# A two-layer decoder trunk on one core: normalised tokens kept in the residual's column order, a shorter rank computation and finer filler units ahead of the expert stage

## The chip, the cores and the metric

The kernel runs on one core of one Trainium2 chip. The metric is the device time of the whole launch in microseconds (us), the median of several executions.

## What is computed

Two layers over 256 tokens of width 1024, batch 1. Each layer is a mixer (a gated short convolution beside block-sparse attention, which with 256 tokens is plain causal attention) and then a hierarchical mixture of experts. Only the second matters here. Cut to it:

```
h2 = rmsnorm(x, norm2_g[l]) * (1.0 + scale2) + shift2
g_logits = t @ w_rg + b_rg                      # 4 groups
g_sel    = argmax(g_logits)
e_logits = (t @ w_re + b_re).reshape(n, 4, 4)   # 4 experts in each group
top_v, top_i = top_k(e_logits[tok, g_sel], 2)
w_sel    = softmax(top_v) * g_prob[tok, g_sel]
hid = silu(t @ w_gate[e]) * (t @ w_up[e])       # D 1024 -> F 256, 16 experts
y   = sum over the chosen experts of combine * hid @ w_down[e]
x   = x + gate2 * y
```

All inputs and outputs are float32. Where two logits are equal, the lower index wins, in `argmax` and in `top_k`.

## The kernel before, in words

All weights are streamed once, in an order written out by hand (`stream`), through ten slots of 1 MB in SBUF (`raw`); SyncE issues the loads and waits before each for the slot's last reader (`wait_free`). Each layer runs: projections, attention, output projection, and then the router and the experts. Every engine has its own hand-written program, and semaphores tie them together.

**Router.** After the output projection, TensorE transposes the residual (`res_transposes`, line 1697; it takes every fourth column, stride 4, because the weight rows lie in SBUF as "partition p holds rows 4p to 4p+3 of a half"). It multiplies by the router weights (`router_rows`, line 1704) and adds four partial rows (line 1740). VectorE forms the logits `lg` (line 1228), compares all pairs in each set of four (lines 1234 to 1239), sums to ranks (line 1240) and gets the assignment `asg` (line 1245). TensorE turns `asg` into places (lines 1745, 1747, 1750) and VectorE builds the selection matrices `sel` (line 1256), 64 slots for each expert. Between these steps TensorE is given filler work, `late_units`: products of the modulation weights that must be done at some time anyway (line 1410 in layer 0, kind "A", eight units; line 1402 in layer 1, kind "G2", four units of twice the matmuls).

**Normalised tokens.** ScalarE writes the high part `xn_hi` (a rounded fp32r copy of the residual times its scale, line 717) and VectorE the low part `xn_lo` (what rounding left, line 1195). Both read the residual with a stride of 4 floats and write it permuted: the 128 columns of feature block k lie side by side. `xn_low(0, ...)` runs while row 1 of the residual is still being made; `xn_low(1, 0, 2)` stands behind the assignment, `xn_low(1, 1, 3)` behind the first quarter of `sel`.

**Experts.** Sixteen experts go in eight pairs. `gather(q, g)` (line 1766) multiplies the normalised tokens by `sel` to put the features of quarter q's tokens in columns. Its stationary operand is a 128x128 block of `xn_hi` or `xn_lo`, its moving operand 256 columns of `sel`:

```
ins = pe.matmul(ps[:, bank, j * S:(j + 1) * S], xn[part][:, t, k * P:(k + 1) * P],
                sel[:, t, 256 * q:256 * (q + 1)], ...)
```

One call is 8 matmuls; there are 16 calls in a layer, four in a row for quarter 0 and then one between the other steps of pairs 0 to 5. `gate_up` (line 1786), `hid_transpose` (line 1795), `down` (line 1812) and `scatter` (line 1828) make up the rest of a pair. ScalarE turns each gathered piece into `hg` (line 755). Before the first pair's second half come the transposes of `sel` (line 1854) and the combine weights (line 1863).

`ada_cols` (line 1445) is a small product whose stationary operand is a 128x128 float32 block of `mod_rows`: for kind "A" with columns side by side, for kind "M" with every fourth column (`mod_rows[:, j::4]`).

Of the kernel before, what the change touches and what calls it, by code (L numbers as in the profile page):

```python
# [13 lines left out]
P = 128  # L14
# [8 lines left out]
BIG = 4096.0  # L23
RING = 6
# [7 lines left out]
def trunk(nc, x, c, positions, norm1_g, norm2_g, w_ada, b_ada, w_in, conv_w, q_norm_g, k_norm_g,  # L32
# [31 lines left out]
    with ExitStack() as ctx:  # L64
# [371 lines left out]
        def _(pool):  # L436
# [15 lines left out]
            for i in range(1, EG):  # L452
                pool.memset(tri[:, i, 0:i], 1.0)
# [59 lines left out]
        def _(act):  # L513
# [103 lines left out]
            for l in range(L):  # L617
# [97 lines left out]
                def xn_high(t, h0, h1):  # L715
                    cols = slice(512 * h0, 512 * h1)
                    act.activation(xn_hi[:, t, cols].rearrange("p (h k q) -> p h k q", h=h1 - h0, k=4),
                                   res[:, t, cols].rearrange("p (h q k) -> p h k q", h=h1 - h0, k=4),
                                   ACT.Copy, scale=stat[:, t:t + 1]).then_inc(xhi_ready, 1)
# [112 lines left out]
        def _(dve):  # L832
# [165 lines left out]
            for l in range(L):  # L998
# [193 lines left out]
                def xn_low(t, h, n):  # L1192
                    cols = slice(512 * h, 512 * (h + 1))
                    dve.wait_ge(xhi_ready, 3 * l + n)
                    dve.scalar_tensor_tensor(out=xn_lo[:, t, cols].rearrange("p (k q) -> p k q", k=4),
                                             in0=res[:, t, cols].rearrange("p (q k) -> p k q", k=4),
                                             scalar=stat[:, t:t + 1],
                                             in1=xn_hi[:, t, cols].bitcast(F32).rearrange("p (k q) -> p k q", k=4),
                                             op0=ALU.mult, op1=ALU.subtract).then_inc(xlo_ready, 1)
# [25 lines left out]
                dve.tensor_copy(logit4[:, P:2 * P], ps[:, 0, 0:P]).then_inc(rows_dve, 1)  # L1225
                dve.wait_ge(logit_done, l + 1)
                for t in range(T):
# [6 lines left out]
                dve.tensor_tensor(beat, other, own, ALU.is_gt)  # L1234
                link(dve.tensor_tensor(tie, other, own, ALU.is_equal))
                link(dve.tensor_tensor(tie, tie,
                                       tri[:, :, :].unsqueeze(1).to_broadcast([P, T * (NG + 1), EG, EG]),
                                       ALU.mult))
                link(dve.tensor_tensor(beat, beat, tie, ALU.add))
# [10 lines left out]
                xn_low(1, 0, 2)  # L1250
# [3 lines left out]
                for q in range(NQ):  # L1254
                    es = slice(4 * q, 4 * q + 4)
                    dve.tensor_tensor(sel.rearrange("p t (e s) -> p t e s", s=SLOTS)[:, :, es, :],  # L1256
                                      slots[:, 0:SLOTS].unsqueeze(1).unsqueeze(1).to_broadcast([P, T, 4, SLOTS]),
                                      slot_of[:, :, es].unsqueeze(3).to_broadcast([P, T, 4, SLOTS]),
                                      ALU.is_equal).then_inc(sel_ready, 1)
                    if q == 0:  # L1260
                        xn_low(1, 1, 3)
# [125 lines left out]
        def _(pe):  # L1387
            def ada_acc(kind, l, ks):
# [6 lines left out]
                for k in ks:  # L1395
                    unit = ("a", q, k)
                    pe.wait_ge(raw_full[ring_slot[unit]], landed[unit])
                    if kind in ("G1", "G2"):
                        for j in range(2):
                            for i in range(4):  # L1400
                                c0 = j * D + 256 * i
                                ins = pe.matmul(ps[32 * i:32 * i + 32, 6, 0:256], c_rep[:, 2 * k + j, :],  # L1402
                                                raw[:, ring_slot[unit], c0:c0 + 256],
                                                start=(k == 0 and j == 0), stop=(k == 3 and j == 1),
                                                skip_group_check=True)
                        ins.then_inc(ada_used, 1)
                        continue
# [100 lines left out]
            def layer(l):  # L1508
# [199 lines left out]
                def late_units(first, last):  # L1708
                    if l + 1 < L:
                        ada_acc("A", l + 1, range(2 * first, 2 * last))  # L1710
                    else:
                        ada_acc("G2", l, range(first, last))
# [17 lines left out]
                res_transposes(1, 6, 8, 2)  # L1730
                pe.wait_ge(tokT_dve, l + 1)
# [3 lines left out]
                late_units(0, 1)  # L1735
# [7 lines left out]
                late_units(1, 3)  # L1743
# [9 lines left out]
                late_units(3, 4)  # L1753

                xn = (xn_hi, xn_lo)

                def gather(q, g):
# [4 lines left out]
                    for j in range(2):  # L1762
                        k = 2 * g + j
                        for t in range(T):
                            for part in range(2):
                                ins = pe.matmul(ps[:, bank, j * S:(j + 1) * S], xn[part][:, t, k * P:(k + 1) * P],  # L1766
                                                sel[:, t, 256 * q:256 * (q + 1)], start=(t == 0 and part == 0),
                                                stop=(t == T - 1 and part == 1))
# [124 lines left out]
                def every_expert():  # L1893
# [3 lines left out]
                    for k in range(KD):  # L1897
                        for t in range(T):
                            c0 = (k % 2) * S + t * P
                            ins = pe.transpose(ps[:, k // 2, c0:c0 + P], tokmaj[:, t, k * P:(k + 1) * P], ident[:, :])  # L1900
# [72 lines left out]
```

## Time and profile before

| | us |
|---|---|
| median of 3 runs | 551.92 (551.55 to 552.21) |
| the profiled execution's own time | 551.99 |
| its span, first to last instruction | 550.2 |
| TensorE matmul busy | 534.3 (97% of the span) |
| TensorE weight load busy | 346.6 (63%) |
| VectorE busy | 299.2 (54%) |
| ScalarE busy | 222.7 (40%) |
| moved from HBM | 188.12 MB, 344 GB/s over the span |
| mean granted TensorE clock | 0.994 |

Busy times of TensorE are modelled at their ends and overlap (a 256-column matmul is shown with 283 ns while the next starts 120 ns later). So the pace of TensorE is read here from start to start. The expert stages lie at about 161 to 285 us and 418 to 546 us.

### The profile page before, as it was taken

Reading aid. Unit: us, or ns where it says so; the run is one execution under the profiler, and the core shown is the slowest. Engines: PE = TensorE matmul, PEld = TensorE weight load, DVE = VectorE, ACT = ScalarE, POOL = GpSimd, SP = SyncE. Lnnn points to the kernel's source line nnn. Section 1 sums busy time; section 2 is a strip of 40 time slices with the busy share of each in tenths; the row PEclk is TensorE's granted clock in tenths of the full one; section 3 lists DMA queues with packets and bytes.
Section 4 is the critical chain, followed back from the end, with each engine's and each line's share of the span. In section 5 each row is a group of like instructions: output and inputs, shape, how many; then the busy total and the mean of one; then the engine's idle time right before and its main releaser. Section 6 shows DMA issues by size and latency. Waiting matters only on the chain.

```text
span 550.2 us, 8078 instructions
## 1 busy us (share of the span) xinstructions
PE 534.3 (97%) x3236; PEld 346.6 (63%) x3236; DVE 299.2 (54%) x502; ACT 222.7 (40%) x384; POOL 18.2 (3%) x76
## 2 busy tenths in 40 slices
PE   7799999999999999999999999999999999999996
PEld 6568969868755444444357898986875544444333
DVE  3628985899872012222369499499977121112243
ACT  2517555542445322222267365563255422222121
POOL 3104100000000000000000000000000000000000
PEclk9899999999999999999999999999999899999999
DMA  8999999979679999999999943956958799999962
GB/s 299 387 387 365 401 396 416 419 310 395 231 276 413 414 414 413 414 409 418 408 386 388 381 150 116 407 213 255 384 203 304 273 371 399 414 413 415 411 247 80
DMA packets 52222, 189.77 MB, mean 345 GB/s; under 512 B 4722, under 2 KB 4818, under 8 KB 44884
## 3 DMA queue, kind: packets, MB, share of 16 engines
q1 hardware_dynamic: 50784, 185.62, 86.6%
q0 software_dynamic: 1072, 2.45, 1.3%
q10 hardware_dynamic: 324, 1.13, 0.6%
q8 instruction: 28, 0.46, 0.3%
q14 instruction: 14, 0.11, 0.1%
HBM read 188.12 MB, written 1.06 MB: 344 GB/s over the span
## 4 chain that ended last, share of the span: by engine, by line
PE 82%; DVE 10%; ACT 3%; DMA 2%; issue 1%; SPq 1%; ACTq 0%; DVEq 0%
PE ps L1786 20%; PE ps L1543 13%; PE ps L1812 10%; PE ps L1664 8%; PE ps L1550 7%; PE ps L1766 5%; PE ps L1828 5%; PE ps L1410 4%; DMA raw<-in_w_ada_dram 2%; DVE wlo L852 2%; DVE cbc L1099 1%; PE ps L1795 1%; PE ps L1402 1%; SPq L352 1%; DVE work L1324 1%
## 5 line engine op out<-in xcount | busy, mean ns | idle before, releaser
L852 DVE TENSOR_TENSOR wlo<-raw,whi 128x1024 fp32r<-128x1024 f32 x64 | 75.6, 1219 | 15.8 <-ACT whi L547 15.5
L547 ACT ACTIVATE whi<-raw 128x1024 fp32r<-128x1024 f32 x64 | 65.3, 1058 | 24.4 <-PE ps L1543 14.3
L1324 DVE SCALAR_TENSOR_TENSOR work<-ps,cw,work 128x256 f32<-128x256 f32 x16 | 10.9, 682 | 97.5 <-ACT work L793 97.5
L1786 PE MATMUL ps<-raw,qkT 128*64 128x512 f32 x256 | 60.0, 612 | 0.0
L1310 DVE TENSOR_TENSOR v_sb<-ps,gates 128x512 f32<-128x512 f32 x32 | 22.1, 692 | 67.7 <-PE ps L1812 67.7
L1812 PE MATMUL ps<-raw,work 128*64 128x512 f32 x256 | 58.4, 598 | 0.0
L1786 PE MATMUL ps<-raw,cbc 128*64 128x512 f32 x256 | 57.5, 594 | 0.0
L1543 PE MATMUL ps<-act_hi,whi 128*128 128x256 f32 x192 | 55.0, 286 | 0.0
L1543 PE MATMUL ps<-act_hi,wlo 128*128 128x256 f32 x192 | 54.3, 283 | 0.0
L1543 PE MATMUL ps<-act_lo,whi 128*128 128x256 f32 x192 | 54.3, 283 | 0.0
L781 ACT ACTIVATE whi<-v_sb 128x512 fp32r<-128x512 f32 x32 | 20.2, 631 | 56.6 <-DVE v_sb L1310 56.6
L1786 PEld LDWEIGHTS ps<-raw,cbc 128*64 128x64 f32 x256 | 18.0, 137 | 34.8 <-issue 33.7
L1543 PEld LDWEIGHTS ps<-act_hi,whi 128*128 128x128 f32 x192 | 36.8, 192 | 2.5 <-issue 2.3
L1786 PEld LDWEIGHTS ps<-raw,qkT 128*64 128x64 f32 x256 | 17.7, 139 | 32.6 <-issue 29.8
L1543 PEld LDWEIGHTS ps<-act_hi,wlo 128*128 128x128 f32 x192 | 36.8, 192 | 0.1
L1812 PEld LDWEIGHTS ps<-raw,work 128*64 128x64 f32 x256 | 17.1, 136 | 31.3 <-issue 30.6
L1543 PEld LDWEIGHTS ps<-act_lo,whi 128*128 128x128 f32 x192 | 36.8, 192 | 0.0
L1766 PEld LDWEIGHTS ps<-whi,act_hi 128*128 128x128 f32 x128 | 24.2, 189 | 19.4 <-issue 18.6
L1550 PE MATMUL ps<-whi,act_hi 128*128 128x512 f32 x88 | 34.8, 396 | 0.2 <-DVE wlo L852 0.2
L1766 PE MATMUL ps<-whi,act_hi 128*128 128x256 f32 x128 | 34.3, 303 | 0.2 <-DVE whi L1256 0.2
L1550 PE MATMUL ps<-wlo,act_hi 128*128 128x512 f32 x88 | 34.3, 389 | 0.0
L1550 PE MATMUL ps<-whi,act_lo 128*128 128x512 f32 x88 | 34.3, 389 | 0.0
(267 smaller groups left out, 880.1 us busy)
## 6 DMA issues: line engine op xcount, KB each, us to landing
raw<-in_w_ada_dram SPq DMA_DIRECT2D x40, 1024.0 KB, 10.2
raw<-in_w_gate_dram SPq DMA_DIRECT2D x64, 512.0 KB, 7.3
raw<-in_w_up_dram SPq DMA_DIRECT2D x64, 512.0 KB, 9.1
raw<-in_w_down_dram SPq DMA_DIRECT2D x32, 1024.0 KB, 10.7
raw<-in_w_in_dram SPq DMA_DIRECT2D x23, 1024.0 KB, 14.3
raw<-in_w_ada_dram SPq DMA_DIRECT2D x16, 512.0 KB, 11.6
raw<-in_w_out_dram SPq DMA_DIRECT2D x8, 1024.0 KB, 5.9
res<-in_x_dram ACTq DMA_DIRECT2D x1, 1024.0 KB, 5.0
```

The costliest lines, as they stand in the source:

```text
L547: act.activation(whi[:, slot(n), :], raw[:, r, (i % 2) * 1024:(i % 2 + 1) * 1024], ACT.Copy).then_inc(hi_done, 1)
L781: act.activation(y_hi[:, cols], y_f[:, cols], ACT.Copy).then_inc(yhi_ready, 1)
L852: dve.tensor_tensor(wlo[:, slot(n), :], raw[:, ring_slot[("w", l, i // 2)], (i % 2) * 1024:(i % 2 + 1) * 1024], whi[:, slot(n), :].bitcast ...
L1310: dve.tensor_tensor(y_f[:, cols], ps[:, 2 + n, :], gates[:, 1, cols], ALU.mult).then_inc(yg_ready, 1)
L1410: ins = pe.matmul(ps[32 * i:32 * i + 32, 6, :], c_rep[:, row, :], raw[:, ring_slot[unit], i * 512:(i + 1) * 512], start=(k == 0), stop=(ki ...
L1543: ins = pe.matmul(ps[:, bank + j // 2, (j % 2) * S:(j % 2 + 1) * S], w[pw][:, kk * 512 + j * P:kk * 512 + (j + 1) * P], acts[pa][:, k, :], ...
L1550: ins = pe.matmul(ps[:, bank + t, :], acts[pa][:, k, t * P:(t + 1) * P], w[pw][:, kk * 512:(kk + 1) * 512], start=(k == 0 and p == 0), sto ...
L1664: ins = pe.matmul(ps[:, 2 * t + n, :], acts[pa][:, k, t * P:(t + 1) * P], w[pw][:, n * 512:(n + 1) * 512], start=(k == 0 and p == 0), stop ...
L1766: ins = pe.matmul(ps[:, bank, j * S:(j + 1) * S], xn[part][:, t, k * P:(k + 1) * P], sel[:, t, 256 * q:256 * (q + 1)], start=(t == 0 and p ...
L1786: ins = pe.matmul(ps[i * SLOTS:(i + 1) * SLOTS, 0, :], hg[p // 2 % 2][:, k, c0:c0 + SLOTS], ws[i][:, :, kk, :], start=(k == 0), stop=(k == ...
L1812: ins = pe.matmul(ps[i * SLOTS:(i + 1) * SLOTS, 2 + n, :], hidT[:, p % 2, kk, i * SLOTS:(i + 1) * SLOTS], ws[i][:, c0:c0 + 512], start=(kk ...
L1828: ins = pe.matmul(ps[:, 4 + 2 * t + n, :], selT[:, 2 * p + t, :], ys[part][:, n * 512:(n + 1) * 512], start=(p == 0 and part == 0), stop=( ...
```

## The change

Five edits, all between the output projection and the experts or in the gather.

1. `xn_high` and `xn_low` read and write in the residual's own column order. The matmuls of `gather` then take their stationary operand with a stride of 4 floats (`feature_block(k)`: every fourth column of a half). A rarely run path, `every_expert`, does the same; it doesn't run with these inputs.
2. Ranks: `beat = (other > own) + (other == own) * tri` in four operations becomes `tie = other - own`, `beat = tie > tri` in two, with `tri` holding the smallest normal float, negated, where it held 1.
3. `xn_low(1, 0, 2)` moves from behind the assignment to the place ahead of the wait for the logits, and `xn_low(1, 1, 3)` from behind the first quarter of `sel` to where `xn_low(1, 0, 2)` stood.
4. `late_units` counts in eighths. In layer 0 an eighth is one unit of "A"; in layer 1 it is half a unit of "G2" (`ada_acc` takes `js`, and counts a unit as used only with its second half).
5. The filler is laid out as 1, 1, 3 and 3 eighths, the first of them ahead of the router rows of k = 4, 5; before, it was 2, 4 and 2 eighths, all behind the router rows.

```diff
-                pool.memset(tri[:, i, 0:i], 1.0)
+                pool.memset(tri[:, i, 0:i], -LEAST)
...
-                    act.activation(xn_hi[:, t, cols].rearrange("p (h k q) -> p h k q", h=h1 - h0, k=4),
-                                   res[:, t, cols].rearrange("p (h q k) -> p h k q", h=h1 - h0, k=4),
-                                   ACT.Copy, scale=stat[:, t:t + 1]).then_inc(xhi_ready, 1)
+                    act.activation(xn_hi[:, t, cols], res[:, t, cols], ACT.Copy, scale=stat[:, t:t + 1]
+                                   ).then_inc(xhi_ready, 1)
...
-                    dve.scalar_tensor_tensor(out=xn_lo[:, t, cols].rearrange("p (k q) -> p k q", k=4),
-                                             in0=res[:, t, cols].rearrange("p (q k) -> p k q", k=4),
...
+                    dve.scalar_tensor_tensor(out=xn_lo[:, t, cols], in0=res[:, t, cols], scalar=stat[:, t:t + 1],
+                                             in1=xn_hi[:, t, cols].bitcast(F32), op0=ALU.mult, op1=ALU.subtract
+                                             ).then_inc(xlo_ready, 1)
...
                 dve.tensor_copy(logit4[:, P:2 * P], ps[:, 0, 0:P]).then_inc(rows_dve, 1)
+                xn_low(1, 0, 2)
                 dve.wait_ge(logit_done, l + 1)
...
-                dve.tensor_tensor(beat, other, own, ALU.is_gt)
-                link(dve.tensor_tensor(tie, other, own, ALU.is_equal))
-                link(dve.tensor_tensor(tie, tie,
-                                       tri[:, :, :].unsqueeze(1).to_broadcast([P, T * (NG + 1), EG, EG]),
-                                       ALU.mult))
-                link(dve.tensor_tensor(beat, beat, tie, ALU.add))
+                link(dve.tensor_tensor(tie, other, own, ALU.subtract))
+                link(dve.tensor_tensor(beat, tie, tri[:, :, :].unsqueeze(1).to_broadcast([P, T * (NG + 1), EG, EG]),
+                                       ALU.is_gt))
...
                 res_transposes(1, 6, 8, 2)
+                late_units(0, 1)
                 pe.wait_ge(tokT_dve, l + 1)
...
-                late_units(0, 1)
+                late_units(1, 2)
...
-                late_units(1, 3)
+                late_units(2, 5)
...
-                late_units(3, 4)
+                late_units(5, 8)
...
+                def feature_block(k):
+                    return slice(512 * (k // 4) + k % 4, 512 * (k // 4 + 1), 4)
...
-                                ins = pe.matmul(ps[:, bank, j * S:(j + 1) * S], xn[part][:, t, k * P:(k + 1) * P],
+                                ins = pe.matmul(ps[:, bank, j * S:(j + 1) * S], xn[part][:, t, feature_block(k)],
```

The order of TensorE's instructions in layer 0, from the transposes of the residual's second row to the first gather, before (line 1410 is the filler, a row "x8" of it two units; 1740 the logits, 1745 to 1750 the places and counts):

```order
L1697 MATMUL ps<-ident,res 128x128 x4
L1704 MATMUL ps<-work 32x128 x4
L1410 MATMUL ps<-raw,c_rep 32x512 x8
L1740 MATMUL ps<-r_sum,work 128x20 x2
L1410 MATMUL ps<-raw,c_rep 32x512 x16
L1745 MATMUL ps<-asg,before 128x32
L1747 MATMUL ps<-asg,ones 128x16
L1750 MATMUL ps<-asg,ones 128x16 x2
L1410 MATMUL ps<-raw,c_rep 32x512 x8
```

And with the change (the same instructions under new line numbers):

```order
L1692 MATMUL ps<-ident,res 128x128 x4
L1405 MATMUL ps<-raw,c_rep 32x512 x4
L1699 MATMUL ps<-work 32x128 x4
L1405 MATMUL ps<-raw,c_rep 32x512 x4
L1737 MATMUL ps<-r_sum,work 128x20 x2
L1405 MATMUL ps<-raw,c_rep 32x512 x12
L1742 MATMUL ps<-asg,before 128x32
L1744 MATMUL ps<-asg,ones 128x16
L1747 MATMUL ps<-asg,ones 128x16 x2
L1405 MATMUL ps<-raw,c_rep 32x512 x12
```

One filler unit now stands between the transposes and the router rows; the logits have one unit ahead of them where they had two; the places follow three units where they followed four; the gather follows three where it followed two.

VectorE in the same place, before, from the copy of the second router row to the second quarter of `sel`:

```order
L1225 COPY work<-ps 128x128
L1228 SCALAR_TENSOR_TENSOR lg<-ps,stat,oh 128x20 x2
L1234 TENSOR_TENSOR work<-lg 128x160
L1235 TENSOR_TENSOR work<-lg 128x160
L1236 TENSOR_TENSOR work<-work,tri 128x160
L1239 TENSOR_TENSOR work<-work 128x160
L1240 TENSOR_REDUCE rnk<-work 128x40
L1242 TENSOR_SCALAR goh<-rnk 128x8
L1245 SCALAR_TENSOR_TENSOR asg<-rnk,goh 128x32
L1249 TENSOR_SCALAR slot_of<-asg 128x32
L1195 SCALAR_TENSOR_TENSOR act_lo<-res,stat,act_hi 128x512
L1252 TENSOR_TENSOR slot_of<-slot_of,ps 128x32
```

And with the change:

```order
L1223 COPY work<-ps 128x128
L1195 SCALAR_TENSOR_TENSOR act_lo<-res,stat,act_hi 128x512
L1227 SCALAR_TENSOR_TENSOR lg<-ps,stat,oh 128x20 x2
L1233 TENSOR_TENSOR work<-lg 128x160
L1234 TENSOR_TENSOR work<-work,tri 128x160
L1236 TENSOR_REDUCE rnk<-work 128x40
L1238 TENSOR_SCALAR goh<-rnk 128x8
L1241 SCALAR_TENSOR_TENSOR asg<-rnk,goh 128x32
L1245 TENSOR_SCALAR slot_of<-asg 128x32
L1195 SCALAR_TENSOR_TENSOR act_lo<-res,stat,act_hi 128x512
L1248 TENSOR_TENSOR slot_of<-slot_of,ps 128x32
L1252 TENSOR_TENSOR whi<-slots,slot_of 128x2x256 x4
```

A low part (line 1195) has moved up ahead of the logits, two of the four pair operations are gone, and the four quarters of `sel` follow one another. ScalarE, SyncE and GpSimd issue the same instructions in the same order as before.

## Rows read from the trace of the kernel before

**Rows 1.** The page: the span, and each engine's busy time.
```profile
span 550.2 us, 8078 instructions
PE 534.3 (97%) x3236; PEld 346.6 (63%) x3236; DVE 299.2 (54%) x502; ACT 222.7 (40%) x384; POOL 18.2 (3%) x76
```

**Rows 2.** The page: shares of the chain that ended last, by engine.
```profile
PE 82%; DVE 10%; ACT 3%; DMA 2%; issue 1%; SPq 1%; ACTq 0%; DVEq 0%
```

**Rows 3.** Waits in 165 to 283 us: waiter, releaser, total us, times, longest.
```profile
PEld ps L1795 <- DVE work L1324: 1.1, 3, 0.5
...
SPq L381 <- PE ps L1786: 35.5, 8, 8.0
```

**Rows 4.** The gather's weight loads, by source line: duration in ns, least/median/most.
```profile
L1766 PEld LDWEIGHTS ps<-whi,act_hi x128: 186/189/192, 161.2 to 505.6; 128*128 128x128 f32 x128
```

**Rows 5.** The gather's line in two windows: window, its length, PE and PEld busy (instructions), clock, DMA share, GB/s.
```profile
161.24:165.06 3.82, 3.82 (x32) 3.82 (x32) 1.00 1.02 414
183.25:184.39 1.14, 1.14 (x8) 0.93 (x8) 1.00 1.03 410
```

**Rows 6.** Weight loads in order of time (start, us, what): stride 4 at 143 us, contiguous at 165 us.
```profile
143.34 1.94 PEld L1445 LDWEIGHTS ps<-rowsel,mod_rows 128*128 128x128 f32 x8
144.99 1.23 PEld L1697 LDWEIGHTS ps<-ident,res 128*128 128x128 f32 x8
146.13 0.20 PEld L1664 LDWEIGHTS ps<-whi,act_hi 128*128 128x128 f32 x1
...
165.06 0.98 PEld L1445 LDWEIGHTS ps<-rowsel,mod_rows 128*128 128x128 f32 x8
166.06 0.20 PEld L1786 LDWEIGHTS ps<-raw,qkT 128*64 128x64 f32 x4
```

**Rows 7.** Loads of the small modulation product by source line: ns, least/median/most.
```profile
L1445 PEld LDWEIGHTS ps<-rowsel,mod_rows x24: 192/318/332, 143.3 to 404.7; 128*128 128x128 f32 x24
```

**Rows 8.** The chain: transposes with a contiguous stationary operand.
```profile
77.78 1.90 PE ps L1582 x16
```

**Rows 9.** The timeline at 427 us: contiguous fp32r loads ahead of 4-column matmuls.
```profile
427.50 1.86 PEld L1863 LDWEIGHTS ps<-comb_parts,whi 128*128 128x128 f32 x16 [0.34 <-DVE comb_parts L1293]
```

**Rows 10.** Layer 0 ahead of the gather, TensorE in order of time [idle before <-releaser].
```profile
150.83 0.75 PE L1697 MATMUL ps<-ident,res 128*128 128x128 f32 x4
151.95 0.57 PE L1704 MATMUL ps<-work 128*32 128x128 f32 x6 [0.37 <-DVE work L1210]
154.82 3.64 PE L1410 MATMUL ps<-raw,c_rep 128*32 128x512 f32 x32
161.24 0.39 PE L1766 MATMUL ps<-whi,act_hi 128*128 128x256 f32 x1
```

**Rows 11.** Layer 1 ahead of the gather, VectorE and TensorE in order of time.
```profile
412.53 0.29 DVE L1225 COPY work<-ps 128x128 f32<-128x128 f32 x1 [0.56 <-PE ps L1704]
413.86 0.38 DVE L1228 SCALAR_TENSOR_TENSOR lg<-ps,stat,oh 128x20 f32<-128x20 f32 x2 [1.05 <-PE ps L1740]
414.28 0.33 DVE L1234 TENSOR_TENSOR work<-lg 128x160 f32<-128x160 f32 x1
415.60 0.32 DVE L1240 TENSOR_REDUCE rnk<-work 128x40 f32<-128x160 f32 x1
416.40 0.41 PE L1745 MATMUL ps<-asg,before 128*128 128x32 f32 x2 [0.71 <-DVE asg L1245]
417.40 1.07 PE L1402 MATMUL ps<-raw,c_rep 128*32 128x256 f32 x16
418.72 0.36 PE L1766 MATMUL ps<-whi,act_hi 128*128 128x256 f32 x1 [0.25 <-DVE whi L1256]
```

**Rows 12.** Groups by form: the high and low parts, and a contiguous row of the low part's kind.
```profile
L1195 DVE SCALAR_TENSOR_TENSOR act_lo<-res,stat,act_hi 128x512 fp32r<-128x512 f32 x8 | 9.0, 1146 | 0.1
L1099 DVE SCALAR_TENSOR_TENSOR cbc<-cg,mix_col,cbc 128x256 f32<-128x256 f32 x16 | 7.8, 485 | 0.6
```

**Rows 13.** Windows of one us: PE busy (instructions), granted clock, DMA share, GB/s.
```profile
431.00:432.00 1.00, 1.00 (x4) 0.50 0.97 397
```

More of the change, by code:

```diff
@@ L23 @@
 BIG = 4096.0
+LEAST = float(np.finfo(np.float32).tiny)
 RING = 6
@@ L1194, in xn_low @@
                     dve.wait_ge(xhi_ready, 3 * l + n)
-                    dve.scalar_tensor_tensor(out=xn_lo[:, t, cols].rearrange("p (k q) -> p k q", k=4),
-                                             in0=res[:, t, cols].rearrange("p (q k) -> p k q", k=4),
-                                             scalar=stat[:, t:t + 1],
-                                             in1=xn_hi[:, t, cols].bitcast(F32).rearrange("p (k q) -> p k q", k=4),
-                                             op0=ALU.mult, op1=ALU.subtract).then_inc(xlo_ready, 1)
+                    dve.scalar_tensor_tensor(out=xn_lo[:, t, cols], in0=res[:, t, cols], scalar=stat[:, t:t + 1],
+                                             in1=xn_hi[:, t, cols].bitcast(F32), op0=ALU.mult, op1=ALU.subtract
+                                             ).then_inc(xlo_ready, 1)
                 xn_low(0, 0, 1)
@@ L1249, in _ @@
                 link(dve.tensor_scalar(slot_of[:, :, :], asg[:, :, :], -BIG, BIG, ALU.mult, ALU.add))
-                xn_low(1, 0, 2)
+                xn_low(1, 1, 3)
                 dve.wait_ge(place_done, l + 1)
@@ L1259, in _ @@
                                       ALU.is_equal).then_inc(sel_ready, 1)
-                    if q == 0:
-                        xn_low(1, 1, 3)
                 link(dve.scalar_tensor_tensor(out=oh1[:, :, :].rearrange("p t (g e) -> p t g e", e=EG),
@@ L1387, in _, with ada_acc @@
         def _(pe):
-            def ada_acc(kind, l, ks):
+            def ada_acc(kind, l, ks, js=(0, 1)):
                 q = chunk_of[(kind, l)]
@@ L1398, in ada_acc @@
                     if kind in ("G1", "G2"):
-                        for j in range(2):
+                        for j in js:
                             for i in range(4):
@@ L1405, in ada_acc @@
                                                 skip_group_check=True)
-                        ins.then_inc(ada_used, 1)
+                        if js[-1] == 1:
+                            ins.then_inc(ada_used, 1)
                         continue
@@ L1709, in late_units @@
                     if l + 1 < L:
-                        ada_acc("A", l + 1, range(2 * first, 2 * last))
+                        ada_acc("A", l + 1, range(first, last))
                     else:
-                        ada_acc("G2", l, range(first, last))
+                        for n in range(first, last):
+                            ada_acc("G2", l, (n // 2,), (n % 2,))
                 pe.wait_ge(row_added, 4 * l + 2)
@@ L1899, in every_expert @@
                             c0 = (k % 2) * S + t * P
-                            ins = pe.transpose(ps[:, k // 2, c0:c0 + P], tokmaj[:, t, k * P:(k + 1) * P], ident[:, :])
+                            ins = pe.transpose(ps[:, k // 2, c0:c0 + P], tokmaj[:, t, feature_block(k)], ident[:, :])
                     ins.then_inc(x_in, 1)
```

## The prediction

> **What bounds the kernel now.** I read the page first. TensorE's matmuls are shown busy for 97% of the span [rows 1], which alone proves little, since their ends are modelled; but the chain of waits runs over TensorE for 82% of the span, and over DMA for 2% [rows 2]. So from there on I read TensorE from start to start. Next, the waits in the expert stage of layer 0 (165 to 283 us): SyncE, which issues the weight loads, waits 35.5 us for one line of TensorE alone, and TensorE's only wait on another engine of any size is 1.1 us, for VectorE's product ahead of the hidden transposes [rows 3]. No row there has TensorE waiting for a load. The DMA queues are full as well (share 1.02, 414 GB/s [rows 5]), so the two are close to balance, but it is TensorE that is waited for. The expert stages are therefore priced instruction by instruction on TensorE: whatever lengthens one there lengthens the run, unless it falls into one of the few gaps.
>
> **The stationary operand of the gather, now with stride 4.** This is the large term. A layer has 16 calls of 8 matmuls, 128, and the kernel 256. Today 32 of them start within 3.82 us, 0.119 us each [rows 5]. A later call of 8 takes 1.14 us: 8 x 0.119 = 0.95, and 0.19 for changing over from and to other work. What a load costs by itself is seen where the matmul behind it has only 4 columns: 16 contiguous fp32r loads take 1.86 us, (1.86 - 0.19)/15 = 0.111 us each [rows 9]. So the gather already runs close to the pace of its loads, and a slower load isn't hidden.
>
> No fp32r load with a stride is in the trace. The nearest is the small modulation product, which is there in both kinds: with columns side by side 8 loads go from 165.06 to 166.06, 0.125 us each; with every fourth column, from 143.34 to 144.99, 0.206 us each [rows 6]. Their durations are 192 ns at least and 318 ns in the median [rows 7], 16 of the 24 being the strided ones. The gather's loads last 186 to 192 ns [rows 4], like the contiguous ones of that product, so I take them to be the same kind and to go to 0.206 us. The second kind in the trace is transposes: stride 4 gives (146.13 - 144.99)/8 = 0.143 us [rows 6], contiguous 1.90/16 = 0.119 us [rows 8]. They are further off, since the gather doesn't transpose.
>
> The term: 256 x (0.206 - 0.119) = **+22.2 us**. The bounds: with the transposes' pace 256 x 0.024 = +6.1; if the whole growth of the duration shows, 318 - 192 = 126 ns for each, 256 x 0.126 = +32.3; and if loads stay behind the 256 moving columns, 0. I take 22.2, the row of the same kind and shape.
>
> Two statements of the Trainium skill pull apart here. Its page "SBUF — State Buffer", section "Door 1: The DMA port swizzle", says that consecutive accesses within a 16-byte line run at full bandwidth and each step to a new line pays; a stride of 4 floats makes every access a new line. By that rule, the trace agrees: 0.206 against 0.125 us. The other is among the rivals.
>
> A longer gather fills gaps. After the second gather call of pairs 0 and 1 TensorE waits for the hidden product; that is two of the three waits that sum to 1.1 us [rows 3], 0.7 us a layer, **-1.5 us** in all. From pair 2 on a scatter stands there and nothing is left to fill.
>
> **High and low parts.** The low part of 512 columns takes 1.15 us with the strided read; a contiguous one of that kind and 256 columns takes 0.49 [rows 12], so 512 lie between 0.49 and 0.98. For row 0 both parts lie beside the output projection, for which VectorE waits anyway: 0 us. If that cover were gone they would be earlier, never later. For row 1 see below.
>
> **Layer 0 ahead of the gather.** The transposes start at 150.83 and at 0.143 us each are issued by 151.40; the router rows wait till 151.95 for VectorE's copy [rows 10]. That gap of 0.55 us is now filled with one filler unit. Four units go from 154.82 to the places at 158.39, 0.89 us each, so the router rows come some 0.35 us later and the rest of TensorE's work 0.55 us earlier. Behind them TensorE works without a gap up to the gather at 161.24, and still will: the assignment gets ready earlier than before, and ahead of the places stand three units. The amount of filler is the same. **-0.6 us**.
>
> **Layer 1 ahead of the gather.** The filler here is 64 matmul records, 16 from 417.40, which with its switch to the gather takes under 1 us; I reckon 0.06 each. VectorE's copy ends at 412.53 + 0.29 = 412.82 [rows 11]; the logits could start at 413.02, the filler being shorter there, and `lg` at 413.7 instead of 413.86. The moved low part stands in that wait: from 412.82 it ends by 413.8 at the latest, so it costs at most 0.1. From line 1234 to 1240 four operations take 415.60 - 414.28 = 1.32 us, 0.33 each; two go, -0.66. So the assignment comes about 0.8 us earlier, and the places at 415.6 instead of 416.40. Places and counts take 417.40 - 416.40 = 1.0 us. Behind them stand now 24 records instead of 16, 1.4 us, and the gather starts at 415.6 + 1.0 + 1.4 = 418.0 instead of 418.72; `sel` is ready before that, since VectorE's steps move up with the assignment. What is late next is thus the filler, not VectorE. **-0.7 us**. Two of the four filler units are given back to SyncE later (unit 2 after 417.1 instead of about 415.7 us). The loads behind them are for pairs 0 and 1, a ring of ten slots ahead; SyncE waits for TensorE there anyway: 0.
>
> Behind each gather the chain over ScalarE (line 755), the exponentials and the combine weights starts from the gather's end, as before: 0.
>
> **The sum**, against the profiled execution's own 551.99 us, which is 0.07 above the median of the runs: +22.2 - 1.5 - 0.6 - 0.7 = +19.4, **571.4 us**.
>
> **The rivals.**
>
> *Hidden loads (faster).* The stride costs nothing because a load runs behind the 256 columns of the matmul before it. For it: today's pace of 0.119 us is hardly above the bare load's 0.111, and the stages ahead do get shorter. Then only -0.6 and -0.7 are left: 550.7 us. It decides if a strided load takes no more than about 0.12 us. Against it: 0.206 measured for the same shape. Chance 0.15.
> The Trainium skill's page "TensorE: Matmul & The Clock Gate", section "LDWEIGHTS (loading the stationary operand)", gives the time of a load by its columns alone, columns/1.2 ns, 107 ns here, with no word of a stride. By that rule the time would be this rival's 550.7; the trace disagrees with it in the 0.206 us of the small product, and no run here has yet shown it for the gather.
>
> *The transposes' pace (slower, less).* +6.1, gaps filled by at most 0.2 us at four places, -0.8, and the -1.3 ahead: 556.0 us. For it: a strided load costs one fixed extra, whatever the kind. Against: the product's extra of 0.08 us is more than three times that of the transposes. Chance 0.14.
>
> *DMA is the bound.* Shares are at 1.02, so a slower TensorE could only use up slack, and the time would stay at 551.9. Against: SyncE waits for TensorE and not the reverse [rows 3]. Chance 0.03.
>
> *The whole duration shows.* +32.3 - 1.5 - 1.3 = 581.5 us. Chance 0.02.
>
> *The clock.* At 431 us TensorE is granted 0.50 of full speed [rows 13], the lower of its two levels, for a stretch of some 3.4 us behind thin work ahead of the experts; that costs 1.7 us. With the gather paced by loads the matmuls get thinner still, so a second such stretch may come (+1.7), or this one may go (-1.7). This widens every case, and moves none.
>
> **How the numbers follow.** The forecast has a chance of 0.66, with a range of its own from 565 to 578 us (loads at 0.18 to 0.23 us, clock 1.7 either way). Range: 555 to 580, which takes in the transposes' pace and leaves out the hidden loads, the DMA case and the whole duration, 0.20. A difference of 0.2% (1.1 us) is about what a measurement of this kernel can tell from none. Faster 0.15, within it 0.03, slower 0.82.
>
> **What would show it.** In the profile of the changed kernel: loads of the gather last about 320 ns and not 189; 32 gather matmuls take 6.6 us and not 3.82; a call of 8 takes 1.8 us; the pairs with a gather grow by 1.4 us and those without stay; the gather of layer 0 starts 0.6 us earlier and that of layer 1 0.7 us earlier; the four pair operations become two. I am wrong if the loads last 189 ns, or if they last 320 and the pace stays at 0.12.

## The result and the profile after

The changed kernel takes 580.81 us (median of 4 runs, 580.24 to 583.55) where the kernel before takes 552.07 (4 runs): a ratio of 1.0527, 95% interval 1.0501 to 1.0553, 28.7 us more. The direction and the mechanism were forecast, the size was not: 571.4 us, with a range that ended at 580.

The page of the changed kernel: span, busy times and the chain's shares.

```profile
span 578.4 us, 8075 instructions
PE 563.4 (97%) x3236; PEld 375.1 (65%) x3236; DVE 294.8 (51%) x498; ACT 218.2 (38%) x384; POOL 18.4 (3%) x76
...
PE 86%; DVE 8%; ACT 2%; DMA 2%; issue 1%; SPq 1%; ACTq 0%; DVEq 0%
```

Against [rows 1, 2] the busy share of TensorE says nothing, 97% both times. The weight loads are busy for 28.5 us more, the chain's share of TensorE has grown from 82 to 86%, and VectorE and ScalarE do less.

The gather's loads by source line, and its first 32 matmuls as a window (length, PE and PEld busy, clock, DMA share, GB/s); these answer to [rows 4, 5].

```profile
L1766 PEld LDWEIGHTS ps<-whi,act_hi x128: 307/329/334, 160.9 to 533.6; 128*128 128x128 f32 x128
L1766 PE MATMUL ps<-whi,act_hi x128: 390/396/514, 160.9 to 533.7; 128*128 128x256 f32 x128
```

```profile
160.90:168.49 7.59, 7.59 (x32) 7.55 (x32) 1.00 1.02 416
```

A load now lasts 329 ns, not 189. 32 matmuls take 7.59 us, 0.237 each, not 3.82. The whole list of waits for 165 to 297 us shows no wait of TensorE for a DMA. SyncE's waits for TensorE have grown, as against [rows 3]:

```profile
SPq L382 <- PE ps L1786: 44.5, 8, 11.7
```

The stretches, from start to start of the same instructions. "Ahead" is from TensorE's last transposes of the residual to the first gather matmul, "experts" from there to ScalarE's table load of the next layer (285.52 us before, 299.90 after) or to the end of the span.

| stretch | before | after | difference |
|---|---|---|---|
| start to the last transposes of layer 0 | 150.83 | 151.18 | +0.35 |
| ahead, layer 0 | 10.41 | 9.72 | -0.69 |
| experts, layer 0 | 124.28 | 139.00 | +14.72 |
| table load to the last transposes, layer 1 | 125.10 | 125.14 | +0.04 |
| ahead, layer 1 | 8.10 | 7.34 | -0.76 |
| experts, layer 1, and the end | 131.48 | 146.02 | +14.54 |

The sum is 28.2 us, the difference of the spans. The first row lies ahead of everything that the change touches; two executions of one kernel differ by more than that there (150.94 and 150.48 us, the last kernel below).

The gather's first 32 matmuls with what they take up to the next product, in the chain: before, and with the change.

```profile
161.31 4.03 PE ps L1766 x32
```

```profile
160.97 7.68 PE ps L1766 x32
```

The two stretches ahead of the gather, TensorE and VectorE in order of time; they answer to [rows 10, 11].

```profile
151.18 0.75 PE L1692 MATMUL ps<-ident,res 128*128 128x128 f32 x4
151.86 1.06 PE L1405 MATMUL ps<-raw,c_rep 128*32 128x512 f32 x8
152.74 0.40 PE L1699 MATMUL ps<-work 128*32 128x128 f32 x8
...
158.19 2.78 PE L1405 MATMUL ps<-raw,c_rep 128*32 128x512 f32 x24
160.90 0.51 PE L1766 MATMUL ps<-whi,act_hi 128*128 128x256 f32 x1
```

```profile
427.16 0.75 DVE L1195 SCALAR_TENSOR_TENSOR act_lo<-res,stat,act_hi 128x512 fp32r<-128x512 f32 x1
...
428.01 0.39 DVE L1227 SCALAR_TENSOR_TENSOR lg<-ps,stat,oh 128x20 f32<-128x20 f32 x2
428.43 0.33 DVE L1233 TENSOR_TENSOR work<-lg 128x160 f32<-128x160 f32 x1
...
429.14 0.32 DVE L1236 TENSOR_REDUCE rnk<-work 128x40 f32<-128x160 f32 x1
...
429.95 0.41 PE L1742 MATMUL ps<-asg,before 128*128 128x32 f32 x2 [0.55 <-DVE asg L1241]
...
430.95 1.50 PE L1396 MATMUL ps<-raw,c_rep 128*32 128x256 f32 x24
432.38 0.51 PE L1766 MATMUL ps<-whi,act_hi 128*128 128x256 f32 x1
```

In layer 0 a filler unit stands in the former gap, and the gather follows straight behind the filler. In layer 1 the low part (0.75 us, 1.15 before [rows 12]) ends at 427.91, 0.1 us ahead of the logits; the pair operations take 0.71 us where they took 1.32; and again it is the filler that the gather follows.

### The profile page after: what moved, and what is told of

Same layout as the page of the kernel before. It is cut to its first block, busy times and chain, and to the rows that moved or that the text cites. A ratio compares the mean times of both kernels' runs of the same rounds, so it can differ in the third digit from the quotient of the medians.

```text
span 578.4 us, 8075 instructions
## 1 busy us (share of the span) xinstructions
PE 563.4 (97%) x3236; PEld 375.1 (65%) x3236; DVE 294.8 (51%) x498; ACT 218.2 (38%) x384; POOL 18.4 (3%) x76
## 4 chain that ended last, share of the span: by engine, by line
PE 86%; DVE 8%; ACT 2%; DMA 2%; issue 1%; SPq 1%; ACTq 0%; DVEq 0%
PE ps L1786 19%; PE ps L1538 12%; PE ps L1766 11%; PE ps L1812 10%; PE ps L1659 8%; PE ps L1545 7%; PE ps L1828 4%; PE ps L1405 4%; DMA raw<-in_w_ada_dram 2%; DVE wlo L852 2%; DVE cbc L1099 1%; PE ps L1396 1%; PE ps L1692 1%; PE ps L1440 1%; DVE stat L1069 1%
## 5 line engine op out<-in xcount | busy, mean ns | idle before, releaser
L1766 PEld LDWEIGHTS ps<-whi,act_hi 128*128 128x128 f32 x128 | 41.7, 326 | 19.1 <-issue 19.1
L1766 PE MATMUL ps<-whi,act_hi 128*128 128x256 f32 x128 | 53.6, 419 | 0.0
L1766 PE MATMUL ps<-whi,act_lo 128*128 128x256 f32 x128 | 50.8, 397 | 0.0
L1766 PEld LDWEIGHTS ps<-whi,act_lo 128*128 128x128 f32 x128 | 42.4, 331 | 0.0
L1786 PEld LDWEIGHTS ps<-raw,qkT 128*64 128x64 f32 x256 | 17.7, 140 | 33.1 <-issue 29.9
```

The costliest lines, as they stand in the source:

```text
L1786: ins = pe.matmul(ps[i * SLOTS:(i + 1) * SLOTS, 0, :], hg[p // 2 % 2][:, k, c0:c0 + SLOTS], ws[i][:, :, kk, :], start=(k == 0), stop=(k == ...
```

## The experiments

The theory: every strided load costs about 0.117 us more than a contiguous one, wherever it stands, and nothing else makes the run longer. The rivals: the load got slower only together with the 256 moving columns; part of the loss is the new order of filler and low parts; the stride as such is slow, or only the step from line to line.

**The price of a load.** Two kernels that hold nothing but rows of matmuls.

> Computes nothing of the reference: only rows of 8 to 16 matmuls, each row with one kind of stationary operand (128x128) and one width, read for their pace from start to start. Theory A (the load alone sets the pace, I read it too short in the trace of before): fp32r with stride 4 goes at 0.23 us at 4 columns and at 256 columns alike, and at 512 columns it is nearly hidden (0.23 against the 0.22 of a contiguous one). Theory B (the load takes 0.206 and the moving columns slow it further): 0.206 at 4 columns, 0.235 at 256. On the stride: if a 16-byte line is what counts, stride 2 lies at or near the contiguous 0.11 to 0.12, stride 3 between, stride 4 and 8 alike at 0.23; if any stride but 1 is a slow kind, stride 2 is at 0.23 too. Alternating strided and contiguous at 256 columns: the mean of both, 0.175 us. A strided moving operand: no expectation with a number, 0.12 if it is free.

Its rows followed one another under one source line and merged in the profile, so nothing could be read off it. The second kernel sets them apart with contiguous 512-column matmuls between:

```diff
+            warm(140)
+            for j in range(16): pe.matmul(ps[:, 0, 0:4], wr[:, 0:128], mr[:, 0:4], start=True, stop=True)
+            warm(16)
+            for j in range(16): pe.matmul(ps[:, 0, 0:4], wr[:, 0:255:2], mr[:, 0:4], start=True, stop=True)
...
+            for j in range(16): pe.matmul(ps[:, 0, 0:256], wr[:, 0:509:4], mr[:, 0:256], start=True, stop=True)
```

> As the first probe, with 16 contiguous 512-column matmuls between the rows so that each row can be read apart and TensorE stays busy; it computes nothing of the reference. From the run with stride 2, whose gather went at the contiguous pace, I now expect stride 2 at or near the contiguous one at 4 and at 256 columns. Theory A (the load alone): stride 4 at 0.235 us at 4 columns and at 256. Theory B (load and moving columns together): 0.206 at 4 columns, 0.235 at 256. Stride 3 between 2 and 4; 8 like 4. At 512 columns stride 4 at 0.235 or below, contiguous 0.22. Alternating: 0.175 us in the mean. bf16: stride 4 (8 bytes) near contiguous, stride 8 (16 bytes) slow.

Weight loads of this kernel in order of time (start, us of the 16 together, line): at 4 columns stride 1, 2, 3, 4, 8; at 256 columns stride 1, 2, 4; and last at 256 columns every second load strided.

```profile
40.25 1.98 PEld L75 LDWEIGHTS ps<-mr,wr 128*128 128x128 f32 x16
45.73 2.07 PEld L77 LDWEIGHTS ps<-mr,wr 128*128 128x128 f32 x16
51.26 2.91 PEld L79 LDWEIGHTS ps<-mr,wr 128*128 128x128 f32 x16
57.63 3.81 PEld L81 LDWEIGHTS ps<-mr,wr 128*128 128x128 f32 x16
64.92 3.88 PEld L83 LDWEIGHTS ps<-mr,wr 128*128 128x128 f32 x16
73.85 2.09 PEld L85 LDWEIGHTS ps<-mr,wr 128*128 128x128 f32 x16
79.42 2.10 PEld L87 LDWEIGHTS ps<-mr,wr 128*128 128x128 f32 x16
...
91.39 3.81 PEld L91 LDWEIGHTS ps<-mr,wr 128*128 128x128 f32 x16
...
120.72 3.00 PEld L99 LDWEIGHTS ps<-mr,wr 128*128 128x128 f32 x16
```

Each group is 16 busy, overlapping loads. Its last load's duration taken off and divided by 15, with the mean durations 191, 327 and 326 ns of lines 75, 81 and 91, this gives 0.119 us for the contiguous load at 4 columns, and for stride 4 0.232 at 4 columns ((3.81 - 0.327)/15) and 0.232 at 256. The moving columns add nothing: theory A holds, B falls. Stride 2 is 0.09 us more for all 16 together, stride 3 halfway (0.18 us a load), stride 8 like 4 (0.236), and the row with every second load strided comes to 0.18, the mean of both kinds. In the changed kernel the gather's matmuls start 0.237 us apart; that last 0.005 us over the bare row, 1.3 us in 256 loads, isn't explained.

Three more rows, as matmuls, stand for other kinds: a contiguous stationary operand with a *moving* operand of stride 4 at 256 columns; and bf16 at 256 columns with stride 4 and 8 (8 and 16 bytes).

```profile
127.43 3.89 PE L101 MATMUL ps<-mr,wr 128*128 128x256 f32 x16
...
160.03 1.94 PE L111 MATMUL ps<-mb,wb 128*128 128x256 bf16 x16
...
165.46 1.97 PE L113 MATMUL ps<-mb,wb 128*128 128x256 bf16 x16
```

The strided moving operand costs as much, 0.23 us for 256 columns. The bf16 rows pace at 0.11 us; with the 16-byte stride their loads last 145 ns where contiguous ones last 98, hidden behind the 256 columns. The row with 16 bytes had been expected to be slow.

**The layout undone, the other four edits kept.**

```diff
-                    act.activation(xn_hi[:, t, cols], res[:, t, cols], ACT.Copy, scale=stat[:, t:t + 1]
-                                   ).then_inc(xhi_ready, 1)
+                    act.activation(xn_hi[:, t, cols].rearrange("p (h k q) -> p h k q", h=h1 - h0, k=4),
+                                   res[:, t, cols].rearrange("p (h q k) -> p h k q", h=h1 - h0, k=4),
+                                   ACT.Copy, scale=stat[:, t:t + 1]).then_inc(xhi_ready, 1)
...
-                                ins = pe.matmul(ps[:, bank, j * S:(j + 1) * S], xn[part][:, t, feature_block(k)],
+                                ins = pe.matmul(ps[:, bank, j * S:(j + 1) * S], xn[part][:, t, k * P:(k + 1) * P],
```

> The change without its first edit: high and low parts in the old permuted layout, gather contiguous. If the layout alone costs, the other four edits leave -0.6 us ahead of the gather of layer 0 and -0.3 to -0.7 us ahead of that of layer 1 (the strided low part of 1.15 us may push the logits there by up to 0.1): 550.7 to 551.2 us, gather matmuls again at 0.119 us. The rival, that part of the loss comes from the new filler order or the moved low parts, gives over 552.

Measured: 553.13 us against 551.98, ratio 1.0016 (1.0006 to 1.0026). The loss of 28.7 us is gone, so it was the layout. But the gain that the other four were to leave isn't there, and the median lies over the 552 us that the rival (a loss from the filler or the low parts) was to give. On the stretches: ahead in layer 0 9.72 us, as forecast; ahead in layer 1 8.11, no gain at all. VectorE there:

```profile
412.25 1.19 DVE L1196 SCALAR_TENSOR_TENSOR act_lo<-res,stat,act_hi 128x512 fp32r<-128x512 f32 x1 [0.45 <-ACT act_hi L718]
413.36 0.37 DVE L1230 SCALAR_TENSOR_TENSOR lg<-ps,stat,oh 128x20 f32<-128x20 f32 x2
```

The strided low part waits 0.45 us for ScalarE's equally strided high part and then takes 1.19 us; the logits, which follow the last transposes by 3.24 us in the kernel before (413.86 - 410.62), follow by 3.75 here. The moved low part doesn't fit into the wait with its reads four floats apart; with contiguous reads it does (and with pairs, below). Its second half (1.14 us) then stands behind the assignment. The stretches explain a gain of 0.6 us, not a loss of 1.1. It was therefore run once more, beside more runs of the kernel before:

> The kernel with the layout undone once more. Its stretches were shorter than before's by 0.69 us and by nothing, yet its median was 1.1 us longer, and 9 of its 12 runs had a mean granted clock of 0.990 or less, 4 of 23 of the kernel before. If its filler order or low parts bring a second lower-clock stretch by their work, most runs are again at 0.990 and the median is again 0.5 to 1.5 us over the kernel before. If that was the state of the chip at that time, it is now at or below the kernel before by up to 0.7 us.

553.12 against 551.96 us, ratio 1.0012 (0.9997 to 1.0027), stretches 9.72 and 8.17. Of its 24 runs in both measurements 18 had a mean granted clock of 0.990 or below, where the kernel before had 4 and 5 of 23 beside them. Sorted by that clock the medians are, in us:

| mean clock | layout undone | before | layout undone, again | before, beside it |
|---|---|---|---|---|
| above 0.990 | 551.54 | 551.94 | 551.25 | 551.83 |
| 0.990 or below | 553.30 | 553.75 | 553.13 | 553.82 |

In each row this kernel is 0.4 to 0.7 us shorter, what its stretches say. It comes out longer in all only because more of its runs have the lower clock. So the rival isn't borne out as a cost of the work itself. Why the lower clock is more frequent isn't shown: a trace stands for one execution of each measurement, and both of these were at 0.996. The one trace at 0.990 is that of the filler alone (below), and there the additional stretch at the lower level lies ahead of everything that was changed, at the start:

```profile
14.00:22.00 8.00, 6.11 (x30) 0.57 1.05 387
```

There the clock is down for some 7 us, where the kernel before and the changed one have it down for 3.4 us at the start, and the layout undone not at all.

**The layout alone**, in the kernel before:

```diff
-                                ins = pe.matmul(ps[:, bank, j * S:(j + 1) * S], xn[part][:, t, k * P:(k + 1) * P],
+                                ins = pe.matmul(ps[:, bank, j * S:(j + 1) * S], xn[part][:, t, feature_block(k)],
```

> The kernel before with the first edit alone. If the layout is the whole loss: 581.5 to 582.5 us, that is, the changed kernel's time plus what the other four edits bring (1 to 1.4), gather matmuls at 0.235 us. If the filler had a part in the loss: below 580.8.

583.07 us, ratio 1.0564 (1.0544 to 1.0585): 2.3 us above the changed kernel, over the expected 0.7 to 1.7. Ahead of the gathers it takes 10.41 and 7.78 us, 0.7 and 0.4 more than the changed kernel. The rest goes with the clock: two of its four runs had a mean of 0.988, and the other two (0.993 and 0.994) take 581.66 and 582.40 us, 1.0 and 1.7 more than the 580.70 in the median of the changed kernel's three at 0.994, as expected. The profile is of a run at 0.988; it has the lower level for some 7 us at the start and once more in pair 0 of layer 0. The contiguous low part by itself shortens layer 1's stretch by 0.3 us, since it stands behind the assignment there.

**Stride two.** High and low parts stored so that a feature block takes every second element; VectorE's instruction is issued in two halves for it.

```diff
-                    return slice(512 * (k // 4) + k % 4, 512 * (k // 4 + 1), 4)
+                    return slice(256 * (k // 2) + k % 2, 256 * (k // 2 + 1), 2)
...
+                        ins = act.activation(xn_hi[:, t, hc].rearrange("p (a q b) -> p a q b", a=2, b=2),
+                                             res[:, t, hc].rearrange("p (q a b) -> p a q b", a=2, b=2),
+                                             ACT.Copy, scale=stat[:, t:t + 1])
```

> The changed kernel with high and low parts stored so that a feature block has stride 2 (8 bytes, two elements to a 16-byte line) and not 4; the writes are permuted in pairs. If the line is what counts, loads last about 190 ns, the gather goes at 0.12 us and the time is that of the run with the layout undone, 551 us. If any stride is slow: 330 ns, 0.235 us, 580 us. Between: a price for every second access, 0.17 us, 565 us.

```profile
L1776 PEld LDWEIGHTS ps<-whi,act_hi x128: 193/195/336, 161.3 to 505.2; 128*128 128x128 f32 x128
```

551.85 us, ratio 0.9994 (0.9976 to 1.0012). The loads are back at 195 ns, the experts at 124.44 and 131.55 us, 0.16 and 0.07 over the kernel before. So it isn't the stride as such that costs. A rule that fits the float32 rows above: a load pays for each element that is alone in its 16-byte line. With strides 1 and 2 none is, with 4 and 8 all are, and with 3 (bytes 0, 12, 24, 36) two of four, at half the price. That is argued, since no run moved where in a line a block starts, and the bf16 row with 16 bytes shows a smaller price (47 ns more for a load, not 136) and the one with 8 bytes a small price where the rule has none (114 ns against 98). And both stretches ahead keep the whole gain, 9.72 and 7.35 us: ScalarE's 512 columns take 776 ns in this layout, where four floats apart they took over 1.2 us. The gain of the stretches shows in the times at like clock: above 0.990 the median is 551.03 us against 551.94, at or below it 552.88 against 553.75. Five of its ten runs are at or below.

**Every second load strided.**

```diff
-                                ins = pe.matmul(ps[:, bank, j * S:(j + 1) * S], xn[part][:, t, feature_block(k)],
+                                ins = pe.matmul(ps[:, bank, j * S:(j + 1) * S],
+                                                xn[part][:, t, feature_block(k) if part == 0 else slice(k * P, (k + 1) * P)],
```

> The changed kernel, but the low parts are stored permuted, so that of the 256 gather loads every second one is contiguous. If each load pays for itself: half of the growth, a pair of matmuls takes 0.235 + 0.119, time about 580.8 - 14.9 = 565.9 us (range 564 to 568). If a strided load hides half behind its contiguous neighbour: less, down to a pace of 0.12 and 552 us. If one strided load throws the pace off for both: near 580.

```profile
161.08 0.51 PE L1770 MATMUL ps<-whi,act_hi 128*128 128x256 f32 x1
...
161.43 0.28 PE L1770 MATMUL ps<-whi,act_lo 128*128 128x256 f32 x1
...
161.78 0.28 PE L1770 MATMUL ps<-whi,act_lo 128*128 128x256 f32 x1
```

565.6 us, ratio 1.0232 (1.0175 to 1.0288), where 565.9 was expected. A pair takes 0.35 us (161.43 to 161.78), the sum of 0.235 and 0.119: each load pays for itself, and no neighbour hides it.

**The gap that wasn't filled.** The changed kernel with one swap on ScalarE:

```diff
-                    if q < NQ:
-                        piece_out(q, 2 * (p % 2) + 1)
                     act.wait_ge(hidT_done, E + 1)
...
                                    ACT.Copy).then_inc(hidT_ready, 1)
+                    if q < NQ:
+                        piece_out(q, 2 * (p % 2) + 1)
```

> The changed kernel with one swap on ScalarE: the copy of the transposed hidden product goes ahead of the second gathered piece of a pair, not behind it. My prediction let the longer gather fill TensorE's wait in pairs 0 and 1 (1.5 us in all); the trace shows the wait in pair 0 still there, now for ScalarE, which does the gathered piece first (1.02 us) and then the copy (0.38). If that queue order is why: 0.8 to 0.9 us less in pair 0 of each layer, up to 0.2 in pair 1, 1.6 to 2.0 us in all, the stretch from the end of pair 0's second gate-up to pair 1's first shorter by that. The rival, that the gap is set by VectorE's product: nothing.

The chain in pair 0 of layer 0, in order of time: the kernel before, the changed one, and this one.

```profile
177.60 0.68 DVE work L1324
...
178.77 0.87 PE ps L1854 x8
179.64 3.60 PE ps L1786 x16
```

```profile
181.29 2.11 PE ps L1766 x8
183.41 0.02 issue
183.43 1.02 ACT cbc L755 x2
184.45 0.28 ACT work L799
184.73 0.04 issue
184.78 3.65 PE ps L1786 x16
```

```profile
181.06 2.10 PE ps L1766 x8
183.16 0.22 PE ps L1795 x2
183.38 0.87 PE ps L1854 x8
184.25 3.58 PE ps L1786 x16
```

Before, TensorE waited for VectorE's product; in the changed kernel it waits for ScalarE, which scales the late piece first and copies second. With the swap TensorE waits for nothing there. From the end of pair 0's second gate-up to pair 1's first it is 3.49 us in the changed kernel and 3.19 here, -0.30, and the same in layer 1 (3.46 and 3.16). The place was right, the size wrong: I had expected 0.8 to 0.9, forgetting that the transposes behind the gather are TensorE's own work. The time is 579.94 us against 580.81, measured with other runs of the kernel before; its ratio to them, 1.05 (1.0446 to 1.0555), doesn't tell the two apart.

**The filler alone and the ranks alone**, each executed once and read by the stretches.

```diff
+                late_units(0, 1)
                 pe.wait_ge(tokT_dve, l + 1)
...
-                late_units(1, 3)
+                late_units(2, 5)
```

> The kernel before with the new filler order alone (edits 4 and 5). From the first of TensorE's last residual transposes to the first gather matmul it is 10.41 us in layer 0 and 8.10 in layer 1 before, 9.72 and 7.34 with the change. I expect the gain of layer 0 to be all from this (9.7), and in layer 1 only part of it, since there VectorE's chain with four pair operations and the low parts still stands behind the assignment: 7.9 to 8.1.

```diff
-                dve.tensor_tensor(beat, other, own, ALU.is_gt)
-                link(dve.tensor_tensor(tie, other, own, ALU.is_equal))
...
+                link(dve.tensor_tensor(tie, other, own, ALU.subtract))
```

> The kernel before with the two-operation ranks alone (edit 2). From TensorE's last residual transposes to the first gather: layer 0 unchanged at 10.41 us, since TensorE's filler is in the way there; layer 1 shorter by 0.3 to 0.66 us from 8.10, since TensorE waits for the assignment there.

Layer 1 with the filler alone, and with the ranks alone:

```profile
411.52 0.75 PE L1698 MATMUL ps<-ident,res 128*128 128x128 f32 x4
...
419.47 0.39 PE L1769 MATMUL ps<-whi,act_hi 128*128 128x256 f32 x1
```

```profile
410.35 0.75 PE L1695 MATMUL ps<-ident,res 128*128 128x128 f32 x4
...
417.85 0.35 PE L1764 MATMUL ps<-whi,act_hi 128*128 128x256 f32 x1 [0.25 <-DVE whi L1254]
```

Filler: 9.72 us in layer 0 (all of that gain) and 7.95 in layer 1. Ranks: 10.41 in layer 0 (nothing) and 7.50 in layer 1, -0.60. In layer 0 TensorE is the one that is full, in layer 1 it waits for VectorE, so the ranks help there alone and the filler mostly in layer 0. In layer 1 filler (-0.15), ranks (-0.60) and the contiguous low part (-0.32) sum to more than the -0.76 of all together: with VectorE's chain shorter, the filler is what is left in the way. The times of these two single executions, 553.31 and 551.11 us, say nothing finer than a stretch at the lower clock.

**A version that beats both:** stride two with the swap.

> The changed kernel with feature blocks of stride 2 and the hidden copy ahead of the gathered piece on ScalarE. Against the kernel before: -0.7 and -0.75 us ahead of the two gathers, +0.2 for slightly slower loads, and -0.1 to -0.3 for each of pairs 0 of both layers from the swap: 1.4 to 1.8 us less on the stretches, 550.3 us, if the clock is granted alike. That is at the edge of what the runs can tell.

550.56 us against 551.86, ratio 0.9976 (0.9958 to 0.9995). Once more:

> The stride-two kernel with the swapped copy once more, beside the same runs of the kernel before: 1.0 to 1.5 us less than before if the first measurement (0.9976, 0.9958 to 0.9995) was no luck; within 0.3 us if it was.

550.40 against 551.96, ratio 0.9978 (0.9961 to 0.9994). Both intervals lie below 1: 1.3 and 1.6 us less than the kernel before. Ahead of the gathers the two profiles show 9.72 and 9.73, 7.38 and 7.35 us. The experts of layer 1 take 129.97 and 129.99 us, 1.5 less than before, because no lower-clock stretch stands in them in either profile; the kernel before has one [rows 13], and this kernel has none there:

```profile
426.00:436.00 10.00, 9.90 (x64) 1.00 0.91 336
```

Taken at like clock (above 0.990) the medians are 550.36 against 551.61 us and 549.98 against 551.83, so 1.3 and 1.9 us less, of which the stretches ahead of the gathers are 1.4. The swap itself adds nothing here: layer 0's experts take 124.41 and 124.40 us, 124.44 without it, since with loads at the old pace TensorE waits for VectorE's product in pair 0 as before. That 0.1 to 0.3 us for each layer, expected of it, was a miss.

## Why the prediction was right or wrong

- **What bounds the kernel:** right. TensorE still waits for no DMA, and of 29.9 us of slower loads the expert stages grew by 29.3.
- **The stride's term, +22.2 us:** the right instructions, the right kind of row, the wrong size. It is +29.9: the first 32 matmuls of layer 0 up to the next product take 7.68 us instead of 4.03 in the chain, +3.65, and layer 1 alike, 7.3 together; 24 calls of 8 take 2.08 us instead of 1.14, 22.6. The step that failed is the pace of a strided load, "from 143.34 to 144.99, 0.206 us each" [rows 6]. I divided the distance to the next group's first load by 8. That load belongs to the transposes and starts only 0.03 us behind the last strided one, for a reason that no run shows. The same row, read as the second kernel of loads was, gives (1.94 - 0.32)/7 = 0.231 us, and 256 x (0.231 - 0.119) = 28.7. The row had the answer; its edge was read as if it were an interval. The right term alone, with the rest of the sum as it stood, gives 579.1 us, still in the range; with the gaps' miss of 1.0 us it is 580.1.
- **The bounds:** 0.143 us (transposes) was too kind, 0.245 (0.119 and all of the growth in duration) too high; what it came to is 0.236 (0.119 + 29.9/256).
- **The gaps that a longer gather fills, -1.5 us:** wrong, it is -0.5. Pair 0 lengthened by 0.93 us in layer 0 and 0.90 in layer 1, nearly a call's full 0.94, pair 1 by 0.70 each. I took the gap as TensorE's alone to fill; behind it ScalarE's queue had the late piece ahead of the copy that TensorE needs. The swap gave back 0.30 us a layer. The other part of the miss is that the gaps were smaller than read: with the swap a call fills 0.31 us in pair 0 (0.94 less 0.63) and 0.24 in pair 1, 0.55 a layer and not 0.7.
- **Layer 0 ahead, -0.6:** measured -0.69, from the filler alone, as argued.
- **Layer 1 ahead, -0.7:** measured -0.76, and the filler is what is late next, as said. That the low part's place costs "at most 0.1" holds with contiguous or pairwise reads, to which I gave no credit: with the old layout the whole gain is gone.
- **The clock:** the changed kernel's profile has the stretch in layer 1 too, at the same place in the work (0.57 of full speed from 448 to 452 us), and the same mean of 0.994; no part of the 28.2 us.
- **The rivals:** hidden loads fell with the first row of the result, and with it the Trainium skill's "TensorE: Matmul & The Clock Gate", section "LDWEIGHTS (loading the stationary operand)", read as if stride did not matter: 0.232 us against 0.119 for the same 128 columns. The Trainium skill's "SBUF — State Buffer", section "Door 1: The DMA port swizzle", says that two hits on a 16-byte line are needed for full bandwidth; the runs agree: stride 2 at 195 ns, stride 4 at 329. Its next sentence lets one stride 4 floats "for free", and there the measurement decides against it.
- **The range** ended at 580 because I gave the whole-duration case 0.02; the bound from above was 0.01 us a load away from what was measured, the central value 0.03.

## What to carry to other kernels

A stationary operand of stride 4 floats moves work from the engines that permute (ScalarE and VectorE, which had time) to the one that is full, and it is paid again in each of 256 loads; a layout in between, with pairs of neighbours and a stride of 2 in the load, kept the gain on both sides. The pace of a group is (busy - last duration)/(n - 1); the distance to a neighbour of another kind isn't an interval. When a longer step is to fill a gap, follow the queue of every engine that works on its result, not only the wait that the gap shows.

## What was not expected of the hardware

A moving operand of stride 4 is as slow as a stationary one: 256 fp32r columns at 0.23 us, not 0.12. A stationary operand of stride 4 behind 512 moving columns is nearly free: 16 matmuls from 113.55 to the next group at 117.31, 0.235 us each, against 0.226 contiguous (106.30 to 109.92). bf16 with a stride of 16 bytes stays at 0.11 us at 256 columns, since its load lasts 145 ns and not 330. And the mean granted clock of a whole run goes with about 2 us: the kernel with the layout undone had 18 of 24 runs at 0.990 or below, the stride-two kernel 5 of 10, and with the swap 3 of 24, at 2.6 and 2.7 us less in the median than with the layout undone. Whether the order of work decides that is open: at 0.990 the one trace there is has its additional stretch ahead of all that was changed.
